# A Mixture-of-Experts kernel on Trainium2: expert lists loaded from GpSimd's own queue, and expert 1's rows turned by TensorE

## What is computed

```python
def ec_moe(h, router_w, w1, w3, w2):
    xt = h.reshape(B * T, D)                       # D = 1024; latent tokens: T = 1024
    cap = EC_FACTOR * (B * T) // N_EXPERTS         # 128 latent tokens, 16 context tokens per expert
    aff = jax.nn.softmax((xt @ router_w).astype(jnp.float32), axis=-1)
    gate_vals, idx = lax.top_k(aff.T, cap)         # each of the 16 experts takes its best tokens
    xe = xt[idx]
    hid = jax.nn.silu(jnp.einsum('ecd,edf->ecf', xe, w1)) * jnp.einsum('ecd,edf->ecf', xe, w3)
    ye = jnp.einsum('ecf,efd->ecd', hid, w2) * gate_vals[..., None]
    y = jnp.zeros_like(xt).at[idx.reshape(-1)].add(ye.reshape(-1, D).astype(xt.dtype))
    return y.reshape(B, T, D)
```

## Time and profile before

| | us |
|---|---|
| median of 3 runs (1629.53 to 1637.18) | 1631.14 |
| the profiled execution | 1631.1 |
| its span on the core | 1629.3 |
| TensorE busy | 1580.3 (97% of the span) |
| DVE busy | 716.6 |
| POOL busy | 477.5 |
| ACT busy | 387.4 |

### The profile page before, as it was taken

One profiled execution on the slowest core, in us unless ns is written; L12 is line 12 of the kernel. 1 busy time (PEld: TensorE's weight loads), 2 busy tenths in 40 slices (PEclk: granted clock), 3 DMA queues, 4 the chain that ended last, 5 costly groups with the idle time before them and its releaser, 6 DMA issues. The chain is left out here.

```text
span 1629.3 us, 28403 instructions
## 1 busy us (share of the span) xinstructions
PE 1580.3 (97%) x11180; PEld 1377.1 (85%) x11180; DVE 716.6 (44%) x1871; ACT 387.4 (24%) x970; POOL 477.5 (29%) x560
## 2 busy tenths in 40 slices
PE   6999999999999899999988999999999999999997
PEld 5866876666668767788878999999999999999997
DVE  4001046776565844222364244444334454433344
ACT  5210113341221466411131111111111111111114
POOL 3000000015232643121203343433344343334432
PEclk9999999999999999999999999999999999999999
DMA  9302212132202486423269899999899999999985
GB/s 346 114 11 85 82 39 59 36 125 30 59 29 93 133 239 204 157 66 103 91 212 353 290 299 297 316 322 298 278 293 304 291 315 329 299 286 285 315 263 228
DMA packets 225582, 324.85 MB, mean 199 GB/s; under 512 B 36015, under 2 KB 116008, under 8 KB 225466
## 3 DMA queue, kind: packets, MB, share of 16 engines
q1 hardware_dynamic: 185817, 282.70, 51.7%
q0 software_dynamic: 15568, 17.45, 5.7%
q10 hardware_dynamic: 24080, 23.02, 4.8%
HBM read 294.42 MB, written 25.51 MB: 196 GB/s over the span
## 5 line engine op out<-in xcount | busy, mean ns | idle before, releaser
L1973 PE MATMUL psum<-arena 128*128 128x144 f32 x4096 | 504.5, 286 | 1.7 <-DVE arena L2615 1.7
L1973 PEld LDWEIGHTS psum<-arena 128*128 128x128 f32 x4096 | 502.8, 190 | 1.9 <-ACT arena L1350 1.9
L1985 PE MATMUL psum<-arena 128*128 128x144 f32 x2048 | 257.3, 288 | 6.3 <-ACT arena L1391 5.0
L1985 PEld LDWEIGHTS psum<-arena 128*128 128x128 f32 x2048 | 254.8, 192 | 7.1 <-ACT arena L1391 5.2
L1556 PE MATMUL psum<-arena 128*128 128x384 f32 x720 | 242.9, 493 | 0.0
L889 POOL DMA_INDIRECT expert_list<-gt x128 | 129.8, 1014 | 317.2 <-DVE gt L2645 287.6
L1556 PEld LDWEIGHTS psum<-arena 128*128 128x128 f32 x720 | 134.5, 191 | 90.0 <-issue 2.9
L2675 DVE TENSOR_TENSOR arena<-gt,psum 128x144 f32<-128x144 f32 x128 | 38.8, 303 | 360.8 <-PE psum L1973 359.8
L2497 DVE SCALAR_TENSOR_TENSOR arena<-arena,gt 128x1024 f32<-128x1024 f32 x128 | 159.1, 1280 | 0.5 <-DMA arena<-affinity_rows 0.5
L1559 PE MATMUL psum<-arena 128*128 128x256 f32 (+2 forms) x784 | 146.4, 346 | 0.0
L1559 PEld LDWEIGHTS psum<-arena 128*128 128x128 f32 x784 | 129.4, 190 | 15.5 <-issue 1.7
(11 more groups left out here) (379 smaller groups left out, 1629.4 us busy)
## 6 DMA issues: line engine op xcount, KB each, us to landing
arena<-in_exp_w SPq DMA_DIRECT2D x96, 2048.0 KB, 11.8
arena<-in_ada_w SPq DMA_DIRECT2D x24, 1024.0 KB, 7.0
arena<-in_w_in SPq DMA_DIRECT2D x11, 1024.0 KB, 5.2
arena<-in_x_sample SPq DMA_DIRECT2D x16, 512.0 KB, 4.8
arena<-affinity_rows SPq DMA_DIRECT2D x16, 512.0 KB
arena<-m_decay_rows ACTq DMA_DIRECT2D x36, 128.0 KB, 3.2
arena<-decay_rows ACTq DMA_DIRECT2D x24, 192.0 KB, 3.4
out<-arena SPq DMA_DIRECT2D x9, 512.0 KB, 2.6
```

Of the source, the lines that this page charges most:

```text
L1973: ins = mm(bank[:, 0:SLOTS], w[:, k, col], xeT[:, k, :], start=(k == 0), stop=(k == KD - 1))
L1985: ins = mm(bk[4 + db % 2][:, 0:SLOTS], wslot[4 + db // 4][:, k, (db % 4) * P:(db % 4) * P + P], hid[:, k, :], start=(k == 0), stop=(k == K ...
```

## The change

List loads leave SP's queue and are issued by POOL. The load of list 1 comes first in the form of one entry to a partition, right behind its scatters; expert 1's tokens are then gathered as whole rows with one indirect DMA, and TensorE turns them, as it does for experts 0 and 15. The quarter form of list 1 is loaded behind that gather. In the loop, list e + 2 is loaded at the end of the pass, behind the wait for the additions. The loop of POOL runs over experts 1 to 12 now, and expert 13 stands by itself, so that list 15 can be loaded in its own form. DVE's wait on the list in `rank_begin` is left out for experts 0 and 1.

```diff
         def listed(e):
-            return 64 * e + 1 if not isinstance(e, int) or e < NE - 1 else 64 * (NE - 2) + 17
+            return 64 * e + 16 if not isinstance(e, int) or e < NE - 1 else 64 * (NE - 2) + 32
         def fetched(e):
-            return 64 * e + 16 if not isinstance(e, int) or e < NE - 1 else 64 * (NE - 2) + 32
+            return 64 * e - 32 if not isinstance(e, int) or e < NE - 1 else 64 * (NE - 3) + 48
...
-            def load_list(e):
-
-                sp.wait_ge(list_sc, 16 * NL * e)
-                if e == NE - 1:
-                    sp.dma_start(lists[:, 8 * e:8 * e + 2], list_d[0:P, :]).then_inc(list_in, 16)
-                    return
-                for c in range(4):
-                    sp.dma_start(lists[32 * c:32 * c + 32, 8 * e:8 * e + 8].rearrange("p (a w) -> p a w", w=2),
-                                 list_d[0:P, :].rearrange("(a i) w -> i a w", i=32)).then_inc(list_in, 16)
...
-            load_list(1)
             load_row(2)
...
                 if e + 1 < NE:
-                    load_list(e + 1)
                     load_row(e + 2)
...
             scatter_list(1)
+            def load_list(e, rows=False):
+                pool.wait_ge(list_sc, 16 * NL * e)
+                pool.sem_inc(idx_set, 1)
+                if rows:
+                    o = 2 if e == 1 else 8 * e
+                    pool.dma_start(lists[:, o:o + 2], list_d[0:P, :]).then_inc(list_in, 16)
+                else:
+                    load_quarters(e)
+            def load_quarters(e):
+                for c in range(4):
+                    dst = lists[32 * c:32 * c + 32, bass.ds(e * 8, 8)].rearrange("p (a w) -> p a w", w=2)
+                    pool.dma_start(dst, list_d[0:P, :].rearrange("(a i) w -> i a w", i=32)).then_inc(list_in, 16)
+            load_list(1, rows=True)
...
             def expert_rows(e, x_rows=False, y_rows=False):
-                pool.wait_ge(list_in, listed(e + 1))
+                pool.wait_ge(list_in, 16 if isinstance(e, int) and e == 0 else listed(e + 1))
                 pool.wait_ge(ex_full, e + 1)
-                pool.wait_ge(xgl_in, fetched(e))
+                pool.wait_ge(xgl_in, 16 if isinstance(e, int) and e == 0 else fetched(e))
                 if x_rows:
-                    pool.tensor_copy(icur[:, 0:1], lists[:, 8 * e + 8:8 * e + 9]).then_inc(idx_set, 3)
+                    o = 2 if e == 0 else 8 * e + 8
+                    pool.tensor_copy(icur[:, 0:1], lists[:, o:o + 1]).then_inc(idx_set, 3)
...
+                if isinstance(e, int) and e == 0:
+                    load_quarters(1)
+                    pool.wait_ge(list_in, listed(1))
                 scatter_list(e + 2)
...
                 pool.wait_ge(sc_l, added(e))
                 pool.sem_inc(e_free, 1)

-            expert_rows(0, y_rows=True)
-            with pool.Fori(1, NE - 2) as e:
+            expert_rows(0, x_rows=True, y_rows=True)
+            load_list(2)
+            with pool.Fori(1, NE - 3) as e:
                 expert_rows(e)
+                load_list(e + 2)
+            expert_rows(NE - 3)
+            load_list(NE - 1, rows=True)
             expert_rows(NE - 2, x_rows=True)
...
-            one_expert(0, y_rows=True)
+            one_expert(0, x_rows=True, y_rows=True)
...
             for e in range(NE - 1):
                 hidden(e)
-                if e == NE - 2:
-                    pe.wait_ge(xgl_in, fetched(NE - 1))
+                if e in (0, NE - 2):
+                    pe.wait_ge(xgl_in, fetched(e + 1))
                     pe.wait_ge(e_yeA, e + 1)
                     pe.wait_ge(e_yeD, e + 1)
                     x_turn_latent(0, KD)
...
-            dve.sem_inc(list_in, 1)
...
             def rank_begin(e):
-                dve.wait_ge(list_in, listed(e - 1))
+                if not isinstance(e, int) or e > 1:
+                    dve.wait_ge(list_in, listed(e - 1))
...
-                    if fb == KD - 2 and not (is_first or is_last or x_rows):
+                    if fb == KD - 2 and not (is_last or x_rows):
                         x_turned(e + 1)
-                if is_first:
-                    x_turned(e + 1)
...
-            expert(0, True)
+            expert(0, True, x_rows=True)
```

More of the change, by code:

```diff
@@ L906, in expert_rows @@
             def expert_rows(e, x_rows=False, y_rows=False):
-                pool.wait_ge(list_in, listed(e + 1))
+                pool.wait_ge(list_in, 16 if isinstance(e, int) and e == 0 else listed(e + 1))
                 pool.wait_ge(ex_full, e + 1)
-                pool.wait_ge(xgl_in, fetched(e))
+                pool.wait_ge(xgl_in, 16 if isinstance(e, int) and e == 0 else fetched(e))
                 if x_rows:
-                    pool.tensor_copy(icur[:, 0:1], lists[:, 8 * e + 8:8 * e + 9]).then_inc(idx_set, 3)
-                else:
-                    quarter_ids(icur[:, 0:4], e + 1, e * 10 + 5)
-                pool.wait_ge(idx_set, e * 10 + 5)
+                    o = 2 if e == 0 else 8 * e + 8
+                    pool.tensor_copy(icur[:, 0:1], lists[:, o:o + 1]).then_inc(idx_set, 3)
+                else:
+                    quarter_ids(icur[:, 0:4], e + 1, e * 11 + 6)
+                pool.wait_ge(idx_set, e * 11 + 6)
                 pool.sem_inc(idx_set, 1)
@@ L927, in expert_rows @@
                 else:
-                    quarter_ids(icur[:, 4:8], e, e * 10 + 11)
-                pool.wait_ge(idx_set, e * 10 + 11)
+                    quarter_ids(icur[:, 4:8], e, e * 11 + 12)
+                pool.wait_ge(idx_set, e * 11 + 12)
                 pool.wait_ge(e_yeA, e + 2)
```

## The result

| | before | after |
|---|---|---|
| time, median of 4 runs (us) | 1632.29 (1629.53 to 1637.18) | 1756.02 (1750.88 to 1758.02) |
| ratio, 95% interval | 1 | 1.075 (1.0714 to 1.0785) |
| span of the profiled execution (us) | 1629.3 | 1756.3 |
| TensorE busy (us), mean granted clock | 1580.3, 0.992 | 1615.9, 0.958 |

The kernel became 7.5% slower. The prediction was 1737, with a range of 1680 to 1775: direction and mechanism held, and the time came out 19 us above the forecast, by a term that the forecast had left out.

What follows compares the result with a forecast made beforehand. TensorE, busy 97% of the span, was taken as the bound. Loop delay 86.4, present stalls -1.9, freer DMA -7.2, clock 32.4, expert 2 0.8, expert 0 -4.5 sum to +106.0 on 1631.1: 1737 us, range 1680 to 1775.

Steps and rivals of the forecast that it cites:

- the slack: Loop chain from additions to token gathers: 1.1 us per expert to spare before TensorE's second products stall.
- The list's trip D: Loop, experts 3 to 14: list issue and landing on POOL delay the chain 8.3 us, ends 5.9 and 10.0.
- The low end of 2.0: Lowest landing time assumed for a POOL list load, from SP's four loads at 871.06; 4.4 us was taken.
- 12 × (8.3 - 1.1): Loop, 12 gathers: the list's delay beyond the spare time recurs in full, adding 86.4 us.
- The clock: Behind each of 12 loop holes TensorE's clock falls to 0.50, costing 2.7 us each, 32.4 in all.
- Expert 2: First gathers ahead of the loop: the list's delay leaves about 0.8 us of loss, 0 to 3.3.
- Expert 0: Expert 1's single whole-row gather, turned by TensorE, shortens the hole: -4.5 us, ends -5.9 and +1.3.
- worth 0: SP's queue: freeing it of list loads and the scatter wait gains nothing, as no TensorE row waits for weights.
- The quick landing: Rival: the list lands quickly on POOL, delay 5.9 us, total 1707 us; chance 0.12.
- The kept clock: Rival: holes come as forecast but TensorE keeps 2.4 GHz, total 1705 us; chance 0.15.
- Congestion: Rival: list pieces queue behind weight packets, delay 13.2 us, total 1796 us; chance 0.07.
- The other side: Rival: slack pays for POOL's round trip and only expert 0's gain shows, 1624.7 us; chance 0.03.

Runs made afterwards that it cites:

- experiment 1: The change with all list loads back on SP, keeping expert 1's whole-row fetch; 1625.29 us, ratio 0.9951 to the kernel before.
- experiment 2: The change with expert 1's list and tokens in quarters as before, lists still on POOL; 1760.75 us, ratio 1.0784 to the kernel before.
- experiment 4: The change with 30 unused identity products on TensorE between hidden and second products of experts 1 to 13; 1734.66 us, ratio 1.0625.
- experiment 9: The change with lists 2 to 14 issued by ScalarE after the additions landed, on a queue without weights; 1765.91 us, ratio 1.0799.
- experiment 10: The change with the first weight transfer of experts 3 to 14 held until the expert's list has landed; 1674.65 us, ratio 1.0254.
- experiment 11: ScalarE issuing the late list loads, with the first weight transfer held until the list has landed; 1680.2 us, ratio 1.0288.
- Experiment 3: The change with list e + 2 issued on POOL ahead of the wait for the additions; 1663.3 us, ratio 1.0188.
- experiment 5: The change with SP's third weight transfer of experts 3 to 14 waiting until the expert's tokens have landed; 1689.78 us, ratio 1.0343.
- experiment 6: The change with lists of experts 3 to 14 loaded by SP after the additions, between second and third weight transfer; 1796.87 us, ratio 1.0999.
- experiment 8: The change with lists back on SP and the third weight transfer held until the tokens have landed; 1625.62 us, ratio 0.9951.
- experiment 7: The change with the list load ahead of the additions' wait and the third weight transfer held until tokens landed; 1651.1 us, ratio 1.0087.

## Why the prediction was right, and where it was 19 us short

**The mechanism.** The lists stand behind the additions, their round trip lies in the chain, the slack is used up, TensorE stops at the 15th second product, and the clock is 0.50 behind the hole. Each step is in the rows of after; experiments 1 and 2 show the cause of the holes, by taking one half of the change away, and experiment 4 that of the slow products. The beat forecast at 56 us is 57.2 (985.98 to 1043.17).

**The list's trip D.** Forecast 8.3, measured 7.76. That the two are so near is in part luck, for its parts were wrong both ways. I gave three issues 3.9, from POOL's pitch for gathers (1.3), but a direct load on POOL has one of 0.59 (2.35 for four), which makes 1.8. And I gave the landing, counted from the fourth issue, 4.4 where it took 6.0. The low end of 2.0 rested on a misreading: of SP's four loads of the earlier trace rows the last was issued at 872.39, not about 873.2, so that its landing took 2.7. The reason I gave for the landing, "the same queue", was half right: experiments 9 and 10 show that the busy DMA engines make it (1.6 behind the last issue without weights, 5.7 with them). The Trainium skill's figure ("DMA: Bandwidth & Descriptors", Anatomy of one DMA, about 2.0 us fixed) fits experiment 10 and not the change, whose lists meet the weights. The Trainium skill says on the same page ("Issuing engines are not separate DMA queues") that DMAs of all issuing engines run on the same 16 and interleave; experiment 9 agrees, with 9.3 us on ScalarE's queue beside the weights and 3.3 in experiment 11 without them.

**The term that was missed.** The prediction took the gathers' landing as it was, 5.65. But with the chain later by 7 us and more they no longer end where the second pair of weights begins; they run beside it, and land in 7.86: 12 × 2.2 = 26.5 us more. That is the step that failed: 12 × (8.3 - 1.1) holds nothing but D. Experiments 3 and 5 show it from the other side (3.0 us in the third pass of 3, ahead of the second pair, and 2.8 in 5, without it). It is not the DMA share as such, which was 1.01 while the gathers landed before and 0.93 after; how the first transfers of a pair slow a gather in flight is not shown. The additions gained 0.9 each, not 0.6; the forecast put that to the longer beat, which no run tests by itself. Together: 7.76 + 2.21 + 0.02 - 0.94 = 9.1 later per expert, less the slack of 1.1, is 8.0; the holes are 7.7 (92.9 - 0.36, over 12).

**The clock.** Forecast 2.7 for each of 12 holes; the 114 products cost 2.6 more in each than 114 × 0.1237. Of that 0.26 comes with any break, at full clock too (14.36 in expert 1), so the clock alone is 2.3, or 28 in all, which is what experiment 4 gives back.

**Expert 2.** Forecast 0.8, measured 0.36.

**Expert 0.** Forecast -4.5, measured -1.4 (55.87 to 54.50). The list landed 5.1 us after its issue (4.4 forecast) and the single gather in 7.0 (6.2). The scatters of its list had landed 1.1 us later as well, counted from the start of the hidden products (874.64 against 871.06). The likely cause stands in SP's row: freed of its wait, it starts expert 1's weights at 866.46, ahead of the list, where before they came behind it, at 874.2.

```profile
866.46 19.34 SPq L639 DMA_DIRECT2D arena<-in_exp_w  x4
...
874.64 0.60 POOL L892 DMA_DIRECT2D gt<-expert_list  x1 [5.39 <-DMA expert_list<-gt]
...
879.75 0.18 POOL L919 CAST gt<-gt 128x1 int32<-128x1 f32 x1 [4.50 <-DMA gt<-expert_list]
...
880.75 1.01 POOL L925 DMA_INDIRECT arena<-h_latent,gt  x1 [0.82 <-POOLq L923]
```

The prediction put this wait at "worth 0", with the contention in its bounds. With the wait, in experiment 1, the hole is 1.27 us in place of 3.85, and the clock isn't lost. But experiment 1 also moves the list load to SP, so what the wait alone is worth is not shown.

**The sum.** In the stretch of the loop the forecast was 86.4 - 1.9 - 7.2 + 32.4 + 0.8 = 110.5, measured 124.2: +26.5 for the gathers, -6.5 for D, -4.1 for the additions, -1.7 for the products behind the holes (12 × 2.56 in place of 32.4), which makes 124.7; what is left (expert 2, a slack 0.3 larger, and 0.15 at each of the 13 breaks, for the 14 products ahead of one end after 1.88 us and not 1.73) nearly cancels. So the miss is small because four errors of either sign partly cancel. Expert 0 makes +3.1. Ahead of the stage 2.5 us and behind it 1.6 came on top, in work that the change doesn't touch. The hidden products of expert 0 start between 848.6 and 855.2 in the thirteen profiled runs, so the 2.5 us are within what runs differ by.

**The rivals.** The quick landing needs free DMA engines, as experiment 10 has them. The kept clock is what experiment 4 shows, with the holes filled. Congestion (D = 13.2) is too much for POOL's queue, but experiment 6 shows it on SP's. The other side, a round trip paid by slack, falls with experiment 1: the gain (5.1 us of the span) is expert 0's, and it shows only without the round trip.

## What to carry to other kernels

What is in flight beside a small transfer, and ahead of it on its queue, counted more here than which engine issued it. A load of a few KB was cheap where nothing large was in flight (4.0 us), and dear in the middle of a prefetch (8 to 15 us). So price a moved DMA by rows that have the traffic of the place it moves to, and price everything behind it in the chain anew as well. A wait that looks like a brake on a prefetch queue can be what keeps the bulk out of the way of a critical small load (experiments 5 and 10 gained 66 and 81 us over the change by adding one, and experiment 8 gained nothing, with the lists in time); look what starts earlier when it goes. And before a load moves behind a wait, count the slack of that chain per pass, since a loop multiplies what is over.

## What the runs showed of the hardware that was not expected

- The same four gathers of 128 rows landed in 2.8 us with the second pair of weights held back, in 5.65 where it began as they ended, and in 7.9 where it began with them. The DMA share meanwhile was 0.32, 1.01 and 0.93. The same four list quarters took 1.6 us from the last issue (DMA share 0.05), 5.7 (share 1.02), and 15.1 from the first one behind 4 MB on their own queue.
- Experiment 3 had two regimes in one run: two passes with 7.7 us of landing, and then ten with 2.8 to 4.4, once the gathers had come ahead of the weights.
- The length of a hole alone does not say whether the clock falls. Behind 1.85 us the 114 products took 15.90 in experiment 11, behind 2.65 in experiment 7 they took 14.37. The windows behind them, of experiment 11 and then of experiment 7 (columns as above), show the mean granted clock:

```profile
995.20:998.00 2.80, 2.80 (x17) 2.80 (x18) 2.77 (x10) 1.84 (x6) 0.00 (x0) 0.74 1.05 409
```

```profile
1280.70:1283.50 2.80, 2.80 (x23) 2.80 (x24) 2.77 (x10) 1.79 (x6) 0.00 (x0) 1.00 0.95 251
```

  What decides between the two stays open.
- POOL issues a direct load in 0.59 us, less than half of an indirect one's 1.3.
